# A change of issue order in an attention loop: TensorE's transposes for the head two steps back ahead of the new head's scores

## What is computed

```python
s_band = jnp.einsum('bnqhgd,bnkhd->bnhgqk', qb, kb).astype(jnp.float32) * scale
s_ctx = jnp.einsum('bnqhgd,bkhd->bnhgqk', qb, k_ctx).astype(jnp.float32) * scale
...
p = jax.nn.softmax(jnp.concatenate([s_band, s_ctx, s_sink], axis=-1), axis=-1)
...
o = (jnp.einsum('bnhgqk,bnkhd->bnqhgd', p_band, vb)
     + jnp.einsum('bnhgqk,bkhd->bnqhgd', p_ctx, v_ctx))
```

## Time and profile before

| | us |
|---|---|
| median of 3 runs | 1762.69 (1761.31 to 1764.1) |
| the profiled execution | 1762.71 |
| its span, first to last instruction | 1760.9 |
| head loop of layer 0, step 2 to the end of Alo | about 298 to 402 |
| head loop of layer 1, the same | about 1259 to 1332 |

### The profile page before, as it was taken

The page is one execution under the profiler, slowest core; times in us unless marked ns, Lnnn a source line. Parts: engine busy times, 40 slices in busy tenths (PEclk is TensorE's granted clock), DMA queues, the critical chain, the costliest instruction groups (busy, mean ns, idle before and its releaser), DMA issues.

```text
span 1760.9 us, 23096 instructions
## 1 busy us (share of the span) xinstructions
PE 1637.2 (93%) x8912; PEld 1411.1 (80%) x8912; DVE 1034.9 (59%) x1462; ACT 573.6 (33%) x912; POOL 563.4 (32%) x312
## 2 busy tenths in 40 slices
PE   6799988989987999999999997997999799999998
PEld 6688877988876888888888886886898688888887
DVE  3758966784766766656656346286553554444442
ACT  1532244661242121221221226233563432222221
POOL 0234654001222222222232223335202344444442
PEclk9799999988998999999999997998899899999999
DMA  7233311102323434444443221221001233333332
GB/s 275 72 120 120 95 55 49 37 13 84 120 81 97 128 96 143 121 120 120 135 124 88 71 60 48 72 78 55 1 1 49 58 98 96 96 95 91 92 93 94
DMA packets 159400, 155.95 MB, mean 89 GB/s; under 512 B 6336, under 2 KB 123728, under 8 KB 159312
## 3 DMA queue, kind: packets, MB, share of 16 engines
q1 hardware_dynamic: 159312, 154.72, 28.7%
HBM read 152.61 MB, written 2.10 MB: 88 GB/s over the span
## 4 chain that ended last, share of the span: by engine, by line
PE 81%; DVE 10%; ACT 4%; issue 3%; DMA 1%; SPq 1%; POOL 0%; DVEq 0%; ACTq 0%; POOLq 0%
PE psA L1618 26%; PE psB L1618 26%; PE ps L1587 3%; PE psS L1286 2%; PE ps L1286 2%; PE psA L1405 2%; PE psA L1406 1%; PE psA L1407 1%; PE psB L1405 1%; PE psB L1407 1%; PE psB L1406 1%; PE psS L1346 1%; DVE Ab L1219 1%; DVE scr L1005 1%; DVE macc L827 1%
## 5 line engine op out<-in xcount | busy, mean ns | idle before, releaser
L448 POOL TENSOR_TENSOR Wlo<-raw,Whi 128x1024 fp32r<-128x1024 f32 x172 | 418.4, 2433 | 1052.4 <-ACT Whi L559 1052.4
L559 ACT ACTIVATE Whi<-raw 128x1024 fp32r<-128x1024 f32 x180 | 190.7, 1060 | 743.1 <-PE psB L1618 333.7
L1219 DVE TENSOR_TENSOR Ab<-Tb 128x768 f32<-128x768 f32 (+1 forms) x64 | 158.7, 2480 | 186.5 <-ACT Tb L768 186.5
L1618 PE MATMUL psA<-Ahi,Whi 128*128 128x512 f32 x480 | 148.9, 365 | 14.5 <-DVE Alo L878 6.1
L1618 PE MATMUL psA<-Alo,Whi 128*128 128x512 f32 x480 | 146.7, 360 | 0.0
L1618 PE MATMUL psA<-Ahi,Wlo 128*128 128x512 f32 x480 | 146.3, 359 | 0.0
L1618 PE MATMUL psB<-Ahi,Whi 128*128 128x512 f32 x480 | 144.7, 356 | 0.0
L1618 PE MATMUL psB<-Alo,Whi 128*128 128x512 f32 x480 | 144.6, 355 | 0.0
L1618 PE MATMUL psB<-Ahi,Wlo 128*128 128x512 f32 x480 | 144.3, 355 | 0.0
L1618 PE MATMUL psA<-Hhi,Whi 128*128 128x512 f32 (+1 forms) x384 | 116.6, 358 | 8.7 <-DVE X L983 8.7
L827 DVE SCALAR_TENSOR_TENSOR macc<-modraw,csil,macc 128x512 f32<-128x512 f32 x112 | 108.9, 1030 | 18.1 <-DMA modraw<-in_w_mod_dram 18.0
(11 more groups left out here) (300 smaller groups left out, 3339.9 us busy)
## 6 DMA issues: line engine op xcount, KB each, us to landing
raw<-in_w_ff_dram SPq DMA_DIRECT2D x128, 512.0 KB, 4.1
modraw<-in_w_mod_dram SPq DMA_DIRECT2D x72, 512.0 KB, 4.2
raw<-in_w_in_dram SPq DMA_DIRECT2D x36, 512.0 KB, 3.7
modst<-in_w_mod_dram SPq DMA_DIRECT2D x16, 512.0 KB, 5.1
raw<-in_w_out_dram SPq DMA_DIRECT2D x16, 512.0 KB, 4.3
modat<-in_w_mod_dram SPq DMA_DIRECT2D x8, 512.0 KB, 3.8
modraw<-in_dft_lat_dram SPq DMA_DIRECT2D x8, 257.0 KB, 3.7
Xin<-in_x_dram SPq DMA_DIRECT2D x4, 512.0 KB, 10.2
```

The source lines that it names most:

```text
L448: nc.gpsimd.tensor_tensor(Wlo[:, s, :], raw[:, s, :], Whi[:, s, :], ALU.subtract).then_inc(S["lo_done"], 1)
L559: nc.scalar.activation(Whi[:, slot, :], raw[:, slot, :], ACT.Copy).then_inc(S["hi_done"], 1)
L1219: V.tensor_tensor(Ab[:, k % 2, 0:w], Tb[:, k % 2, 0:w], Tb[:, k % 2, 0:w], ALU.mult).then_inc(S["h_full"], 1)
L1618: last = mm(dst[:, c0:c0 + cn], wt, x[:, i, c0:c0 + cn], start=f, stop=e)
```

## The change

In `attention(s)` on TensorE the block that issues the transposes of item s-2 is moved from behind the scores of item s to ahead of them, with its waits. Nothing else is touched; the instructions and the semaphore values are the same, and the order on the other engines is unchanged.

```diff
                 elif s == 2:
                     pe.wait_ge(S["g_cent"], l * NT + TT[l])
+                if 2 <= s < n_items + 2:
+                    it = ITEM_FIRST[l] + s - 2
+                    nk = len(KEY_TILES[ITEMS[it][1]])
+                    pe.wait_ge(S["s_exp"], it + 1)
+                    if s >= 3:
+                        pe.wait_ge(S["pt_evac"], it)
+                    for i in range(nk):
+                        last = tr(psS[:, i * P:(i + 1) * P], Pb[:, it % 2, i * P:(i + 1) * P])
+                    last.then_inc(S["pt_ready"], 1)
                 if s < n_items:
                     it = ITEM_FIRST[l] + s
                     _, b, h, k = ITEMS[it]
...
                     last.then_inc(S["s_ready"], 1)
-                if 2 <= s < n_items + 2:
-                    it = ITEM_FIRST[l] + s - 2
-                    nk = len(KEY_TILES[ITEMS[it][1]])
-                    pe.wait_ge(S["s_exp"], it + 1)
-                    if s >= 3:
-                        pe.wait_ge(S["pt_evac"], it)
-                    for i in range(nk):
-                        last = tr(psS[:, i * P:(i + 1) * P], Pb[:, it % 2, i * P:(i + 1) * P])
-                    last.then_inc(S["pt_ready"], 1)
```

## The result

Slower: 1774.1 us, median of five runs (1773.11 to 1781.39), beside 1762.69 us for the kernel before in the same comparison (five runs, 1760.7 to 1764.1). The ratio is 1.0067, 95% interval 1.0045 to 1.0089. The forecast of 1767.5 us had the sign right and the size wrong, and its range (to 1771.5 us) did not hold the time.

A forecast was written before the change was run, and what follows sets the result against it. TensorE was taken to bound most of the head loop, VectorE a stretch of layer 0. Terms 1.5 + 0.4 + 1.85 + 1.05 = +4.8 us, added to 1762.71, gave 1767.5 us; range 1763.5 to 1771.5 us.

The forecast's parts named there:

- layer 0, start and query copy (to V(7)): Layer 0's loop start and block 0's query copy: the step waits longer for copies of probabilities, +0.75 us together.
- layer 0, blocks 1 and 2 (to V(27)): Layer 0's five-key-tile blocks: a later exponential after VectorE's subtraction delays the transposes heading the step, +0.2 us each, +0.4 us.
- layer 0, item 33 (to V(33)): Blocks 3 to 5 of layer 0: item 33's scores now queue behind transposes waiting for a copy, +0.8 us.
- layer 0, low-clock stretch (to exp(45)): Layer 0 at 1.2 GHz, 380.3 to 390 us: scores of items 41 to 44 reach VectorE too late, +0.45 us.
- layer 0, S(47): End of layer 0's loop: item 47's scores wait 1.22 us instead of 0.62 after item 45's exponential, +0.6 us.
- layer 1, start and query copy (to V(7)): Layer 1's loop start and block 0's query copy: the same longer waits for copies, +0.75 us together.
- layer 1, blocks 1 and 2 (to V(27)): Layer 1's five-key-tile blocks: no modulation work on VectorE, half a microsecond of slack left, no loss.
- layer 1, T(29) and T(31): Block 3 of layer 1: transposes of items 29 and 31 come late behind later scores, exponentials and copies, +1.05 us.
- the turn at full speed: Four-key-tile steps: a dependency round of 3.80 us against 3.82 us of TensorE work, no steady loss but no slack.
- Hidden: Head loops: earlier copies hide the waits except at starts and tails, about +1.9 us, 1764.6 us; chance 0.22.
- Clock falls earlier in the loop: Layer 0's loop: new waits drop TensorE's clock some 10 us sooner, +6.5 us on top, 1774 us; chance 0.11.
- Faster: End of layer 0's loop: earlier transposes close a 1.46 us gap and keep the clock up, 1759.0 us; chance 0.05.

The follow-up runs named there:

- again: The changed kernel run again without any edit, beside more runs of the kernel before: median 1774.94 us, ratio 1.0044.
- b_again2: The kernel before, unedited, run as a kernel of its own beside the shared runs of the kernel before: median 1766.41 us, ratio 0.9990.
- the ten products: Ten unused 512-column products on TensorE ahead of layer 1's retention, added to the kernel before: median 1761.45 us, ratio 0.9970.
- after: The first trace of the changed kernel, new order against the kernel before; that profiled execution took 1773.17 us.
- b_again: The kernel before, unedited, run as a kernel of its own beside the shared runs of the kernel before: median 1772.29 us, ratio 0.9999.

## Why the prediction was wrong, and what of it held

**The step that failed** is the last of the sum: "The profiled execution took 1762.71 us (span 1760.9 and 1.8 around it), 0.02 us from the median of the runs, so I add to it directly". Three runs within 3 us of each other looked like a firm base. They stand in the low third of what 177 runs gave, 1758.9 to 1791.3 us with the mean at 1768.6. On that mean the forecast's +4.8 gives 1773.4 us, and the 53 runs of the changed kernel have a mean of 1773.0; as the terms below add up to +2.7 only, part of that agreement is luck. The same slip made the range too narrow: it holds the unknown costs of the edit, but nothing for the clock's stretches outside the loop, which the prediction named as what would make it wrong and to which it gave no term. In the profiled pair the retention at the low clock is 7 of the 10.4 us. There the kernel before stood at the very 1762.69 us of the sum, so what the sum missed in that comparison is the difference: 11.4 us by the medians in place of 4.8. "About 0.2% (3.5 us) is what a measurement of this kernel can tell" was too hopeful for the same reason: with 10 to 12 runs of a kernel beside 31 to 35 the intervals above are 0.23 to 0.38% to either side.

One thing stays open here. The comparison under The result has the two kernels 12.9 us apart by their means, and no later one more than 6.9. If its five runs of the kernel before were drawn like the 172 later ones, all five at 1764.1 us or below would come about once in 250 times (57 of 172 are), and all five of the changed kernel at 1773.11 or above once in 135 (18 of 48 are). So the draw alone is an unlikely account of that comparison; what else was different in it no run shows, and its chip is not on record.

**The terms.** Each is read from the starts of the value products V (L1587), or of the row named, counted from the loop's first L1330, in the trace of `again` less that of before (one of the three whose loop 1 does not start at the low clock):

| term | forecast | measured |
|---|---|---|
| layer 0, start and query copy (to V(7)) | +0.75 | +0.47 |
| layer 0, blocks 1 and 2 (to V(27)) | +0.4 | +0.33 |
| layer 0, item 33 (to V(33)) | +0.8 | +0.83 |
| layer 0, low-clock stretch (to exp(45)) | +0.45 | -0.44 |
| layer 0, S(47) | +0.6 | +0.53 |
| layer 1, start and query copy (to V(7)) | +0.75 | +0.47 |
| layer 1, blocks 1 and 2 (to V(27)) | 0 | -0.41 |
| layer 1, T(29) and T(31) | +1.05 | +0.94 |
| sum | +4.8 | +2.7 |

Where the replay followed rows with the order exchanged it held to about 0.1 us, for T(5), V(33), S(47), T(29) and T(31); max(33) came 0.2 us earlier than forecast. Two things made it too high. One is the low-clock stretch: the clock falls 3.5 us later in the new order (at 383.3 us in place of 379.8), which gives back what was forecast as a loss (low clock in loop 0: 12.9 us in place of 18.5). That is so in all five traces of the new order (12.8 to 13.0 us). Of the four of the old order one (`b_again2`) has it for 14.3 us only, and its loop 0 is 106.4 us, so part of this term is luck of the pair. The other is the turn at full speed. V(24) and V(25) of layer 1 stand 1.91 us apart in the kernel before:

```profile
1316.77 1.00 PE L1587 MATMUL ps<-Pk,PTs 128*128 128x64 f32 x8
1318.68 1.00 PE L1587 MATMUL ps<-Pk,PTs 128*128 128x64 f32 x8
```

and 1.86 us apart in `again`:

```profile
1323.59 1.00 PE L1587 MATMUL ps<-Pk,PTs 128*128 128x64 f32 x8
...
1325.45 1.00 PE L1587 MATMUL ps<-Pk,PTs 128*128 128x64 f32 x8
...
1331.04 0.63 PE L1286 MATMUL psS<-ident,Pb 128*128 128x128 f32 x4 [0.42 <-ACT PTs L727]
...
1334.83 0.63 PE L1286 MATMUL psS<-ident,Pb 128*128 128x128 f32 x4 [0.47 <-ACT PTs L727]
```

That TensorE's "work is unchanged" was not quite so. In four-tile steps scores start 0.35 us behind the transposes (298.29 to 298.64) where value products started 0.44 behind them (302.07 to 302.51), and transposes start 0.84 us behind the value products where scores started 0.81 behind them: a step is 0.05 us shorter. Over layer 1 up to V(27) such steps give back 0.4 us, which the sum had at nothing. The last two rows are T(29) and T(31), which waited for psS as forecast.

Then the clock at the loop's edges, for which there was no term. Behind layer 0 it gives 0.5 us back (loop 0 in `again` is only 1.23 us longer, V(46) is 1.71 us later). Around layer 1 it takes some more: 1.8 us behind the loop in this pair (430.23 against 428.42), at the loop's start in the traces of 80.5 us. Net, +2.7 of waits become +4.05 us in this pair, and +4.1 by the means of all nine traces.

**The rivals.** *Hidden*: the two loops by themselves are +2.8 us, between its +1.9 and the forecast's +4.8, but T(29) to T(31) show that the waits were not hidden. *Clock falls earlier in the loop*: it gave 1774 us, the time that was measured, but by luck: its reason is not there. The clock fell between T(37) at 382.23 us (0.41 us long) and T(38) at 384.31 us (0.66), later than before (380.37), and the loop cost 1.2 us, not 11. The Trainium skill, "TensorE: Matmul & The Clock Gate", section "A second HAM failure mode: psum-queue depth-cycling", which ties frequent short idle gaps between groups of matmuls to a clock that swings, was behind that rival. This case's traces do not bear it out inside the loop: more and longer short gaps ahead of the transposes (12.1 us in place of 1.4) went with less low clock in loop 0. *Faster*: the idle time ahead of the first instruction of that step grew from 1.46 to 1.59 us, as the prediction held against this rival. The low clock in loop 0 did shrink, but loop 0 became longer all the same.

**What the new profile was to show.** Idle time ahead of the transposes, released by PTs, at item 7, near 1324 us (1333.35 in the changed kernel, 0.41 us) and in 363 to 380 us: all there; ahead of T(29) to T(31) of layer 0 it is 0.31 to 1.04 us. Loop 1 longer by 1.8 us: 1.0 in three traces and 2.2 in two. Loop 0 longer by 2.5 to 3.5: 1.1 to 2.1 by pairs of traces, less. No longer wait of the scores: right, 0.0 us.

## What to carry over

An order that puts a step's first instruction behind one more copy costs as long as that copy's buffer is single; a second half of the buffer, if it is free anyway, takes that cost away. Before a sum is added to a time, ask how wide that time is: a run-to-run spread more than four times the sum belongs in the range, and the base needs more than a handful of runs; and a change outside the edited part of a trace should be sought in a second trace of the same kernel before it is put down to the edit.

## What the runs showed of the hardware

- One kernel on one chip took 1758.91 to 1787.29 us in 35 runs. The loops of one order vary by 1.3 us at most among its traces. Over 172 runs of the kernel before, the mean granted clock (0.946 to 0.970) and the time have a correlation of -0.81, so most of the spread goes with the clock, but not all: at a mean clock of 0.966 the runs still lie between 1760.4 and 1770.9 us. The Trainium skill, "TensorE: Matmul & The Clock Gate", section "What's actually happening", holds the number of slow matmuls at a kernel's start to be run-variable and, for modelling, the ramp's cost to be under 1% of a typical span. The spread of whole launches here is 1.6%, so that figure is no bound for it.
- After 3.00 us of idle time the retention of layer 1 starts at 0.50 and may be back at 1.00 after 3 us (22.4 to 24.2 us for the whole, without the ten products) or stay at 0.50 for over 20 us with TensorE busy all the time (31 us in `after`), with the same instructions in the same order.
- Ahead of layer 0's retention TensorE is idle for 2.75 or 2.76 us in each of the nine traces. The granted clock stays at 1.00 through it in the kernel before and in `b_again2`, and falls to 0.50 in `b_again`, the same kernel.
